# Prompt rows normalized and split inside the last sample unit, gate spreads ahead of the output projection, last values loaded into key buffers

## The chip, the cores and the metric

The kernel runs on one core of one Trainium2 chip. The metric is the device time of one execution in microseconds (us). Lower is better. The kernel before takes 1206.15 us in the median of 3 runs (1203.51 to 1208.47).

## The reference

One layer of a hybrid decoder, for a prompt of 512 rows and for 8 sequences of 8 new rows each (64 sample rows) with 2048 cached positions. All data is float32, the width is 1024.

```python
h = x * (1 + scale1) + shift1                 # shift, scale, gate come from c @ w_ada
proj = h @ w_in                               # q, k, v of the mixers A and B
oa = dilated_mix(q_a, k_a, v_a)               # A: 8 heads of 64, windows (128,1), (512,4), (2048,16)
ob = rms_norm(diff_attention(q_b, k_b, v_b, lam), subln_g) * (1 - lam_init)   # B: 4 heads of 2 x 64
mixed = concat(oa, ob) @ w_o
x = layer_norm(ALPHA * x + gate1 * mixed, ln1_g, ln1_b)
u = (x * (1 + scale2) + shift2) @ w_up + b_up
uc = b_conv + sum(ext[:, j:j + S] * w_conv[j] for j in range(3))
y = (gelu(a) * g) @ w_down + b_down           # a, g are the halves of uc
x = layer_norm(ALPHA * x + gate2 * y, ln2_g, ln2_b)
```

The window caches, shifted by 8 rows, the new key and value rows and the last rows of the convolution are outputs too.

## The kernel before

Each engine has its own instruction stream, written out by hand, with semaphores between them. The work of an engine is done in the order in which it is written. The stages are: modulation and input projection; four prompt attention steps; then the sample stage, which the change touches; the output projection with the first norm; the up-projection with convolution; the down-projection with the second norm.

**The sample stage** is a loop over 16 units `sa` (8 sequences, mixer A and B by turns). A unit of mixer A has three groups of cached keys and values, one of mixer B four, of 512 positions (1 MB) each; the last unit, 15, is of mixer B. SP loads the key groups into three buffers `kraw` (`load_keys`); DVE turns them into `ktg` (`turn_keys`, L1211) and counts `kg_t`. POOL loads the value groups into four buffers `vg` (`load_values`, L480), two in `x_sb` and two in `room`; four transfers of 256 KB make up a group, whose page numbers are read first. TensorE scores keys (L1792), turns probabilities (L1842), and weighs values (`weigh_group`, L1823), which counts `sa_vg`. Behind a unit's groups come its new values (L1871), and `sa_pv` counts the unit; ACT takes the result out (`take_out`, into `o_s`, which lies in `o_all`).

The 60 remaining prompt attention steps `pb` are interleaved, four to a unit (`prompt_step`: scores L1725, turn L1730, weighing L1736); their outputs go to `mixv`, in `mix`. After unit 15's prompt steps, all prompt rows of mixer A and B are there.

**The seam behind the last unit**, up to the output projection, is what the change rewrites. In order, on each engine:

- TensorE: weighing of unit 15, sums of the softmax denominators (L1876 to L1878, `sa_l`), turns of prompt features 0 to 3 (`turn_mixed`, L1886; four transposes of 128x128 each), pick products of the sample rows (L1898, `sa_x`), turns of features 4 to 7, sum of squares of the sample rows (L1904), first half of the first projection tile, `spread_gates` (L1919: eight products that spread the gate columns over rows), then the other nine halves. A half is 24 products of 128x512 (`product`, L1656 to L1658: high x high, high x rest, rest x high, over 8 slices k).
- ACT: `take_out`, root of the prompt's mean squares (L964), high parts of the first half of `w_o` (`high_of_wo`, L969, four of 128x1024), copies of the turned features into `ht` (L975, `mt_a`), four more high parts, root for the sample rows (L980), gate copies (L988, `gb_a`).
- DVE: the sample rows are scaled by the denominators (L1372 to L1379, `sa_n`), the prompt rows of mixer B normalized (L1382, L1385, `rms_ok`), the gate columns expanded (L1390, `mt_d`), the picked sample rows copied and squared (L1406 to L1408), then `split_mixed` (L1398 a cast to the high part, L1399 the rest, `mt_rest`) for features 0 to 3 and 4 to 7, and the norm of the sample rows of mixer B (L1412 to L1418), which counts `sa_fin` to 2: the sample rows are placed.
- POOL: the remainders of eight pieces of `w_o` (`rest_of_piece`, L787), one behind each high part; the first four serve the first half of the columns, the others the second.
- SP: `w_o` in two chunks of 2 MB once all keys are scored (`sa_g`); the copies of x once `sa_pv` is 16; the norm rows and the convolution state (L651, L652) once `sa_fin` is 2. TensorE turns the state in eleven small steps (`st_after`, L1954), the first two right behind the second half of the first tile.

The first tile's halves are j = 0 and j = 1; the rest of the stage is paced by TensorE.

```python
            pe.wait_ge(sa_pt, 2 * len(sa))
            pe.wait_ge(pb_pt, len(pb))
            pe.wait_ge(pb_o, len(pb))
            for f in range(4):
                turn_mixed(f)
```

Of the kernel before, what the change touches and what calls it, by code (L numbers as in the profile page):

```python
# [78 lines left out]
def build(nc, a, o, spill):  # L79
# [6 lines left out]
    with ctx:  # L86
# [87 lines left out]
        mt_high_r = part(room_r, 5120, KT_D * NT).rearrange("p (k t) -> p k t", k=KT_D)  # L174
        stage = mix[:, 0:2048].rearrange("p (b n) -> p b n", b=4)
# [34 lines left out]
        ob_t = part(room, 0, 256)  # L210
        ob_q = part(room, 256, 256)
        ob_r = part(room, 512, 256)
# [3 lines left out]
        ln1 = part(room, 1024, 2048).rearrange("p (w d) -> p w d", w=2)  # L216
# [244 lines left out]

        def load_values(eng, w, g):
# [4 lines left out]
            vs = G % NV  # L467
            if G >= NV:
                eng.wait_ge(sa_vg, G - NV + 1)
            if m == 0 and g < 2:  # L470
                for t in range(4):
                    eng.dma_start(vg[vs][t:P:4, :, :],
                                  win_v[:, 4 * g + t, :].rearrange("(i m) f -> m i f", i=4)).then_inc(vg_in[vs], 16)
            elif m == 0:
                for t in range(2):
                    eng.dma_start(vg[vs][t:P:4, :, :],
                                  win_v[96:128, 8 + 4 * t:12 + 4 * t, :]).then_inc(vg_in[vs], 32)
            else:
                for t, pg in enumerate(page_numbers(eng, b, g)):
                    eng.dma_start(vg[vs][t:P:4, :, :],  # L480
                                  flat_v[1][bass.ds(pg, 1)].rearrange("a (i m) h d -> m (a i) (h d)", i=4))\
                        .then_inc(vg_in[vs], 16)
# [3 lines left out]
        def _(sp):  # L486
# [136 lines left out]
            for w in range(1, len(sa) + 1):  # L623
# [12 lines left out]
                elif here:  # L636
                    load_key_tail(sp, w)
            sp.wait_ge(sa_pv, len(sa) - 1)
# [3 lines left out]
            sp.wait_ge(sa_g, NG[len(sa)])  # L642
            for n in range(FIRST_LATE, FIRST_LATE + 2):
                load_chunk(n)
# [57 lines left out]
        def _(pool):  # L702
# [113 lines left out]
        def _(act):  # L816
# [160 lines left out]
            for q in range(4, 8):  # L977
                high_of_wo(q)
            act.wait_ge(sa_q, 1)
            nc.scalar.activation(ob_q, ob_q, ACT.Sqrt).then_inc(sa_r, 1)  # L980

            act.wait_ge(mt_mm, 8)
            for j in range(8):
# [4 lines left out]
                nc.scalar.activation(g[0:rows, kind, CH * half:CH * half + CH], bk(j % 2)[0:rows, :], ACT.Copy)\  # L988
                    .then_inc(gb_a, 1)

# [49 lines left out]
        def _(dve):  # L1040
# [330 lines left out]
            dve.wait_ge(sa_l, 1)  # L1371
            then(nc.vector.reciprocal(l_s, bk(0)[:, 0:16]))  # L1372
            then(nc.vector.tensor_scalar(lam_s[:, 6:7], diff_c[:, 1:2], lam_s[:, 5:6], diff_c[:, 0:1], ALU.mult, ALU.add))
            l_b = l_s.rearrange("p (b m) -> p b m", m=2)
            then(nc.vector.tensor_scalar(l_b[:, :, 1], l_b[:, :, 1], lam_s[:, 6:7], None, ALU.mult))
            dve.wait_ge(sa_o, 16)
            then(nc.vector.tensor_tensor(o_s, o_s, l_s[:, :, None].to_broadcast([P, 16, P]), ALU.mult))
            o_a = o_s.rearrange("p (b m) d -> p b m d", m=2)[:, :, 0, :]
            nc.vector.tensor_tensor(o_a, o_a, colmask[:, None, :].to_broadcast([P, DB, P]), ALU.mult).then_inc(sa_n, 1)  # L1379

            dve.wait_ge(rms_rt, 1)
# [12 lines left out]
            def split_mixed(f):  # L1394

                dve.wait_ge(mt_a, f + 1)
                high = mt_high_r[:, f, 0:SEQ]
                then(nc.vector.tensor_copy(high, ht[:, f, 0:SEQ]))  # L1398
                nc.vector.tensor_tensor(ht_r[:, f, 0:SEQ], ht[:, f, 0:SEQ], high.bitcast(F32), ALU.subtract).then_inc(mt_rest, 1)  # L1399
# [9 lines left out]
            for f in range(4):  # L1409
                split_mixed(f)  # L1410
            dve.wait_ge(sa_sq, 1)
            nc.vector.tensor_scalar(ob_q, bk(3)[:, 0:256], 1.0 / P, EPS, ALU.mult, ALU.add).then_inc(sa_q, 1)  # L1412
            for f in range(4, KT_D):
                split_mixed(f)
# [165 lines left out]
        def _(pe):  # L1580
# [235 lines left out]
            def weigh_group(w, g):  # L1816
                m, b = sa[w]
                G = NG[w] + g
                pe.wait_ge(vg_in[G % NV], v_count(m, w, g))
                for i in range(4):  # L1820
                    for j in range(4):
                        at = P * g + 32 * i + 16 * (j % 2)
                        last = nc.tensor.matmul(bk(4)[32 * j:32 * j + 16, 0:P], pt_s[:, j // 2, at:at + 16],  # L1823
                                                vg[G % NV][:, i, P * j:P * j + P], start=(g == 0 and i == 0),
                                                stop=False, skip_group_check=True)
                last.then_inc(sa_vg, 1)

# [4 lines left out]
            for w, (m, b) in enumerate(sa):  # L1832
# [27 lines left out]
                else:  # L1860
                    prompt_step(PER * w + 1)
                pe.wait_ge(sa_pt, 2 * w + 2)
                pe.wait_ge(sa_ph, w + 1)
                for g in range(len(groups[m])):
                    weigh_group(w, g)
                    if g == 1 and w + 1 < len(sa):
                        prompt_step(PER * w + 3)
                pe.wait_ge(vn_in, 16 * (w + 1))
# [12 lines left out]
            def turn_mixed(f):  # L1881

                if f >= 4:
                    pe.wait_ge(mt_a, f - 3)
# [254 lines left out]
```

## Time and profile before

| what | value |
|---|---|
| median of 3 runs | 1206.15 us (1203.51 to 1208.47) |
| profiled execution, its own time | 1210.44 us |
| its span | 1208.7 us, mean granted TensorE clock 0.929 |
| busy share PE / DVE / POOL / ACT | 87% / 68% / 38% / 22% |
| chain that ended last, by engine | PE 56%, DVE 16%, DMA 10%, issue 8%, SP's queue 5%, POOL 3% |

The span is the time from the first to the last instruction of the profiled execution. Busy shares are averages over stages with different limits; the chain that ended last is followed back from the last instruction, at each step to what released it.

### The profile page before, as it was taken

Reading aid. Unit: us, or ns where it says so; the run is one execution under the profiler, and the core shown is the slowest. Engines: PE = TensorE matmul, PEld = TensorE weight load, DVE = VectorE, ACT = ScalarE, POOL = GpSimd, SP = SyncE. Lnnn points to the kernel's source line nnn. Section 1 sums busy time; section 2 is a strip of 40 time slices with the busy share of each in tenths; the row PEclk is TensorE's granted clock in tenths of the full one; section 3 lists DMA queues with packets and bytes.
Section 4 is the critical chain, followed back from the end, with each engine's and each line's share of the span. In section 5 each row is a group of like instructions: output and inputs, shape, how many; then the busy total and the mean of one; then the engine's idle time right before and its main releaser. Section 6 shows DMA issues by size and latency. Waiting matters only on the chain.

```text
span 1208.7 us, 24024 instructions
## 1 busy us (share of the span) xinstructions
PE 1049.2 (87%) x9389; PEld 846.9 (70%) x9389; DVE 817.2 (68%) x1485; ACT 271.1 (22%) x600; POOL 462.9 (38%) x587
## 2 busy tenths in 40 slices
PE   4699899985888889878857987999999999999993
PEld 2377567764666556556556767999999999776772
DVE  1637445707878778877557576566757677998868
ACT  0300000011433333334323014223232232101001
POOL 0423224312344434443443006456556565433323
PEclk9699999996989999899957996999999999999997
DMA  8948999869899999999751034556786621413102
GB/s 294 405 144 304 343 334 355 306 213 347 289 337 363 369 310 349 348 364 309 255 202 47 36 96 139 209 209 217 258 287 245 244 70 70 153 58 130 63 3 79
DMA packets 100261, 276.54 MB, mean 229 GB/s; under 512 B 9608, under 2 KB 33174, under 8 KB 96549
## 3 DMA queue, kind: packets, MB, share of 16 engines
q1 hardware_dynamic: 83973, 220.42, 51.8%
q0 software_dynamic: 16128, 54.54, 13.0%
q8 instruction: 75, 1.23, 0.4%
q14 instruction: 37, 0.30, 0.1%
q10 hardware_dynamic: 48, 0.05, 0.0%
HBM read 264.60 MB, written 76.69 MB: 282 GB/s over the span
## 4 chain that ended last, share of the span: by engine, by line
PE 56%; DVE 16%; DMA 10%; issue 8%; SPq 5%; POOL 3%; POOLq 1%; ACT 0%; ACTq 0%; DVEq 0%; PEldq 0%
PE wide L1656 16%; PE wide L1657 15%; PE wide L1658 15%; DMA ring<-in_cache_k 4%; DVE ring L1211 3%; PE wide L1792 3%; DMA ring<-in_w_ada 2%; DMA room<-in_w_ada 2%; SPq L615 2%; DMA ring<-in_w_down 1%; PE wide L1604 1%; SPq L458 1%; DVE ring_r L1135 1%; PE wide L1725 1%; PE wide L1736 1%
## 5 line engine op out<-in xcount | busy, mean ns | idle before, releaser
L787 POOL TENSOR_TENSOR ring_r<-ring,ring_r 128x1024 fp32r<-128x1024 f32 x70 | 183.5, 2629 | 225.8 <-DVE ring_r L1095 205.1
L1656 PE MATMUL wide<-x_sb_r,ring_r 128*128 128x288 f32 x704 | 211.2, 300 | 10.6 <-DVE ht_r L1117 7.5
L1657 PE MATMUL wide<-ht_r,ring_r 128*128 128x288 f32 x704 | 209.4, 297 | 0.0
L1658 PE MATMUL wide<-x_sb_r,ring_r 128*128 128x288 f32 x704 | 208.6, 296 | 0.0
L1658 PE MATMUL wide<-ring_r,ht_r 128*128 128x512 f32 (+1 forms) x400 | 159.0, 398 | 0.0
L1656 PEld LDWEIGHTS wide<-x_sb_r,ring_r 128*128 128x128 f32 x704 | 133.5, 190 | 13.6 <-issue 13.6
L1211 DVE STREAM_TRANSPOSE ring<-ring 128x512 f32<-128x512 f32 x208 | 129.1, 677 | 15.5 <-DMA ring<-in_cache_k 14.8
L1658 PEld LDWEIGHTS wide<-x_sb_r,ring_r 128*128 128x128 f32 x704 | 134.2, 191 | 0.0
L1657 PEld LDWEIGHTS wide<-ht_r,ring_r 128*128 128x128 f32 x704 | 133.9, 190 | 0.0
L1656 PE MATMUL wide<-ring_r,x_sb_r 128*128 128x512 f32 (+1 forms) x240 | 97.8, 407 | 8.8 <-DVE ht_r L1117 8.4
L1657 PE MATMUL wide<-ring_r,x_sb_r 128*128 128x512 f32 (+1 forms) x240 | 95.2, 397 | 0.0
L1656 PE MATMUL wide<-ring_r,ht_r 128*128 128x512 f32 (+1 forms) x220 | 88.2, 401 | 4.1 <-DVE ht_r L1477 1.9
L1658 PEld LDWEIGHTS wide<-ring_r,ht_r 128*128 128x128 f32 (+1 forms) x400 | 72.7, 182 | 21.6
L1657 PE MATMUL wide<-ring_r,ht_r 128*128 128x512 f32 (+1 forms) x220 | 86.8, 394 | 0.0
L1491 DVE SCALAR_TENSOR_TENSOR room<-room,vec_t 128x512 f32<-128x512 f32 x44 | 57.6, 1310 | 42.5 <-ACT room L1012 42.5
L1004 ACT ACTIVATE room<-wide,vec_t 128x576 f32<-128x576 f32 x44 | 32.7, 744 | 207.9 <-PE wide L1658 203.1
L1493 DVE SCALAR_TENSOR_TENSOR room<-room,vec_t 128x512 f32<-128x512 f32 x44 | 69.5, 1578 | 1.6
L1736 PE MATMUL wide<-room 128*128 128x128 f32 x320 | 55.5, 308 | 15.9 <-ACT room L909 11.9
L1792 PE MATMUL wide<-ring,x_sb 128*32 128x128 f32 (+1 forms) x1792 | 64.4, 292 | 4.5 <-DVE ring L1211 2.7
L734 POOL TENSOR_TENSOR ring_r<-ring,ring_r 128x512 fp32r<-128x512 f32 x24 | 34.1, 1425 | 88.3 <-ACT ring_r L835 44.5
L480 POOL DMA_DIRECT2D x_sb<-in_cache_v x64 | 35.2, 550 | 84.7 <-issue 83.6
L1095 DVE CAST ring_r<-ring 128x1024 fp32r<-128x1024 f32 x62 | 41.9, 687 | 36.4 <-DMA ring<-in_w_up 30.2
(239 smaller groups left out, 1977.8 us busy)
## 6 DMA issues: line engine op xcount, KB each, us to landing
ring<-in_cache_k SPq DMA_DIRECT2D x128, 256.0 KB
out_wks<-in_cache_win_k SPq DMA_DIRECT2D x8, 4080.0 KB, 19.0
out_wvs<-in_cache_win_v SPq DMA_DIRECT2D x8, 4080.0 KB, 19.8
ring<-in_w_up SPq DMA_DIRECT2D x22, 1024.0 KB, 7.3
room<-in_w_ada SPq DMA_DIRECT2D x8, 2048.0 KB, 10.2
ring<-in_cache_win_k SPq DMA_DIRECT2D x16, 1024.0 KB
room<-in_cache_v POOLq DMA_DIRECT2D x64, 256.0 KB, 5.7
x_sb<-in_cache_v POOLq DMA_DIRECT2D x64, 256.0 KB, 5.1
```

Of the source, the lines that this page charges most:

```text
L480: eng.dma_start(vg[vs][t:P:4, :, :], flat_v[1][bass.ds(pg, 1)].rearrange("a (i m) h d -> m (a i) (h d)", i=4))\
L734: nc.gpsimd.tensor_tensor(rest, w, high.bitcast(F32), ALU.subtract).then_inc(win_pool, 1)
L787: nc.gpsimd.tensor_tensor(rest, w, high.bitcast(F32), ALU.subtract).then_inc(wl_rest, 1)
L1095: nc.vector.tensor_copy(pair_of(n, slice(k, k + 2))[0], slot(SLOT_OF[n])[:, k:k + 2, :]).then_inc(wl_high, 1)
L1211: last = nc.vector.transpose(ktg[:, G % NK, :, 32 * t:32 * t + 32], kraw[G % NK][:, t, :].rearrange("p (g d) -> p g d", d=32))
L1491: then(nc.vector.scalar_tensor_tensor(out=c_p, in0=u_b[:, k % 2, 1:1 + SEQ], scalar=tap(1), in1=c_p, op0=ALU.mult, op1=ALU.add))
L1493: nc.vector.scalar_tensor_tensor(out=c_p, in0=u_b[:, k % 2, 0:SEQ], scalar=tap(0), in1=c_p, op0=ALU.mult, op1=ALU.add)
L1656: nc.tensor.matmul(out, left[0], right[0], start=first, stop=False)
L1657: nc.tensor.matmul(out, left[0], right[1], start=False, stop=False)
L1658: return nc.tensor.matmul(out, left[1], right[0], start=False, stop=last)
L1736: last = nc.tensor.matmul(bank[:, 0:P], pt_b[:, u % 2, P * kb:P * kb + P], vp[:, kb, m, P * (n // 2):P * (n // 2) + P], start=(kb == 0), s ...
L1792: last = nc.tensor.matmul(bank[32 * nn:32 * nn + 32, at:at + nk], qbd[:, w % 2, g].rearrange("p i q -> p (i q)"), keys[:, g, 0:nk], start= ...
```

## The change

Line numbers of the changed kernel differ from those of the kernel before; each move is told by function name here.

- *Last values.* In unit 15 (`LAST`) groups 1 to 3 of the values are loaded by SP, not POOL, into the key buffer `kraw` that has the number of the group, once the key group in it is turned (`kg_t`). They stand on SP's queue between the new values of units 14 and 15. Since these buffers lie in the slots for `w_o`, the `w_o` loads now wait for all weighings too (`sa_vg`).
- *Prompt rows.* TensorE turns features 0 to 3 before the weighing of unit 15, and 4 to 7 between its groups 1 and 2, once the prompt rows are normalized (`rms_ok`). The turned rows go to banks 5, 6, 1, 7, are copied to free parts of `room` (`mt_part`) in place of `ht`, and are split there. DVE splits 0 to 3, normalizes, expands the gate columns and splits 4 to 7 before it scales the sample rows. ACT copies 0 to 3, takes the root, copies 4 to 7, then does `take_out`.
- *Gates.* The eight spreads stand right behind the sums, ahead of the pick products, in banks 5 and 6. ACT's eight high parts of `w_o` come behind them: one behind each of the gate copies 4 to 7, then four more.
- *Places.* `ob_t`, `ob_q`, `ob_r` move in `room`; the norm rows `ln1` move from `room` to `o_all`.

```diff
+        MT_BANK = [5, 6, 1, 7]
+        def mt_part(t, f):
+            return part(t, 9728 + 512 * f if f < 4 else 512 * (f - 4), 512)
...
-        ln1 = part(room, 1024, 2048).rearrange("p (w d) -> p w d", w=2)
+        ln1 = o_all[:, 0:2 * D].rearrange("p (w d) -> p w d", w=2)
...
+        LAST = 2 * DB - 1
+        def v_home(w, g):
+            G = NG[w] + g
+            if w == LAST and g >= 1:
+                return kraw[G % NK].rearrange("p t d -> p (t d)").rearrange("p (i d) -> p i d", i=4)
+            return vg[G % NV]
...
-            if G >= NV:
+            home, landed = v_home(w, g), v_in(w, g)
+            if w == LAST and g >= 1:
+                eng.wait_ge(kg_t, G + 1)
+            elif G >= NV:
                 eng.wait_ge(sa_vg, G - NV + 1)
...
+            for g in range(1, 4):
+                load_values(sp, LAST, g)
             sp.wait_ge(sa_pv, len(sa) - 1)
             load_new_values(sp, len(sa) - 1)
             sp.wait_ge(sa_g, NG[len(sa)])
+            sp.wait_ge(sa_vg, NG[len(sa)])
             for n in range(FIRST_LATE, FIRST_LATE + 2):
                 load_chunk(n)
...
                 for g in range(len(groups[m])):
-                    load_values(pool, w, g)
+                    if w < LAST or g == 0:
+                        load_values(pool, w, g)
```

ACT, behind the loop over the units:

```diff
-            take_out(len(sa) - 1)
-            act.wait_ge(rms_sq, 1)
-            nc.scalar.activation(rms[:, 1, :], rms[:, 0, :], ACT.Sqrt).then_inc(rms_rt, 1)
...
-            for q in range(4):
-                high_of_wo(q)
-            for f in range(KT_D):
-                act.wait_ge(mt_mm, f + 1)
-                nc.scalar.activation(ht[:, f, 0:SEQ], bk(4 + (f + 1) % 4), ACT.Copy, scale=1.0 if f < 4 else g8[:, 0:1])\
-                    .then_inc(mt_a, 1)
...
+            for f in range(4):
+                take_mixed(f)
+            act.wait_ge(rms_sq, 1)
+            nc.scalar.activation(rms[:, 1, :], rms[:, 0, :], ACT.Sqrt).then_inc(rms_rt, 1)
+            for f in range(4, KT_D):
+                take_mixed(f)
+            take_out(len(sa) - 1)
+            act.wait_ge(mt_mm, KT_D)
             for j in range(8):
                 act.wait_ge(gb_mm, j + 1)
...
+                if j >= 4:
+                    high_of_wo(j - 4)
+            for q in range(4, 8):
+                high_of_wo(q)
```

DVE has the lines of `split_mixed` 0 to 3, of the normalization, of the gate columns and of `split_mixed` 4 to 7 ahead of `dve.wait_ge(sa_l, 1)`, in this order, with no line of theirs behind it. TensorE, unit 15 and behind it:

```diff
                 else:
                     prompt_step(PER * w + 1)
+                    pe.wait_ge(pb_min, len(pb))
+                    pe.wait_ge(pb_pt, len(pb))
+                    for f in range(4):
+                        turn_mixed(f)
...
                     weigh_group(w, g)
...
+                    if g == 1 and w + 1 == len(sa):
+                        pe.wait_ge(rms_ok, 1)
+                        for f in range(4, KT_D):
+                            turn_mixed(f)
...
+            pe.wait_ge(mt_d, 1)
+            pe.wait_ge(mt_a, KT_D)
+            for j in range(8):
...
+                    last = nc.tensor.matmul(bk(5 + j % 2)[0:rows, P * c:P * c + P], col, ident[:, :], start=True, stop=True)
+                last.then_inc(gb_mm, 1)
             pe.wait_ge(sa_o, len(sa))
...
+            pe.wait_ge(gb_a, 8)
             pe.wait_ge(mt_a, KT_D)
             for j in range(2 * (TP + 1)):
...
-                if j == 0:
-                    spread_gates()
```

TensorE's order around the last weighing; `wide` are the accumulator banks, `x_sb`, `room` and `ring` hold values, `mix` the prompt rows. Before, from the last two prompt weighings on:

```order
L1736 MATMUL wide3<-room 128x128 x4
L1730 MATMUL wide3<-ident,room 128x128 x4
L1736 MATMUL wide3<-room 128x128 x4
L1823 MATMUL wide2<-x_sb,ht 16x128 x32
L1823 MATMUL wide2<-room,ht 16x128 x32
L1871 MATMUL wide2<-ht 16x128 x4
L1876 MATMUL wide0<-small,sums 128x16
```

Now:

```order
L1864 MATMUL wide2<-ident,mix 128x128 x4
L1864 MATMUL wide3<-ident,mix 128x128 x4
L1864 MATMUL wide0<-ident,mix 128x128 x4
L1864 MATMUL wide3<-ident,mix 128x128 x4
L1852 MATMUL wide2<-x_sb,ht 16x128 x16
L1852 MATMUL wide2<-ring,ht 16x128 x16
L1864 MATMUL wide2<-ident,mix 128x128 x4
L1864 MATMUL wide3<-ident,mix 128x128 x4
L1864 MATMUL wide0<-ident,mix 128x128 x4
L1864 MATMUL wide3<-ident,mix 128x128 x4
L1852 MATMUL wide2<-ring,ht 16x128 x32
L1918 MATMUL wide2<-ht 16x128 x4
```

Both sets of turns (L1864) have moved into the unit, and three of the four value groups are read from `ring`.

ACT's order behind its last prompt copy; `ring_r<-ring` are the high parts of `w_o`, `mix<-wide` the gate copies. Before:

```order
L914 ACTIVATE o_all<-wide 128x128
L964 ACT_TABLE_LOAD
L964 ACTIVATE rms<-rms 128x16
L969 ACTIVATE ring_r<-ring 128x1024 x4
L975 ACTIVATE ht<-wide 128x512 x4
L975 ACTIVATE ht<-wide,g 128x512 x4
L969 ACTIVATE ring_r<-ring 128x1024 x4
L980 ACTIVATE room<-room 128x256
```

Now:

```order
L1000 ACTIVATE rms<-rms 128x16
L989 ACTIVATE room<-wide,g 128x512 x4
L939 ACTIVATE o_all<-wide 128x128
L1010 ACTIVATE mix<-wide 128x512 x2
L1010 ACTIVATE mix<-wide 64x512 x2
L1010 ACTIVATE mix<-wide 128x512
L995 ACTIVATE ring_r<-ring 128x1024
L1010 ACTIVATE mix<-wide 128x512
L995 ACTIVATE ring_r<-ring 128x1024
```

The high parts of `w_o` have moved from ahead of everything to between and behind the last gate copies.

## Rows read from the trace of the kernel before

**Rows 1.** Windows: length, busy us of PE, PEld, DVE, ACT, POOL, PEclk, DMA share, GB/s.

```profile
596.00:612.00 16.00, 6.00 (x117) 4.58 (x119) 1.63 (x9) 0.60 (x1) 3.52 (x7) 0.76 0.96 351
612.00:628.00 16.00, 9.10 (x71) 7.66 (x64) 10.83 (x7) 7.50 (x11) 10.81 (x4) 0.50 0.56 198
628.00:640.00 12.00, 11.97 (x54) 11.13 (x55) 9.93 (x18) 4.17 (x6) 1.90 (x2) 0.57 0.00 0
```

**Rows 2.** Timeline of PE: start us, us, what, xcount [idle before <-releaser].

```profile
598.66 1.94 PE L1823 MATMUL wide<-x_sb,ht 128*16 128x128 f32 x64
...
605.75 1.91 PE L1823 MATMUL wide<-room,ht 128*16 128x128 f32 x32 [5.15 <-DMA room<-in_cache_v]
611.82 1.91 PE L1823 MATMUL wide<-room,ht 128*16 128x128 f32 x32 [4.17 <-DMA room<-in_cache_v]
...
616.80 3.65 PE L1886 MATMUL wide<-ident,mix 128*128 128x128 f32 x16
627.35 7.04 PE L1898 MATMUL wide<-pick,o_all 128*128 128x32 f32 x32 [6.90 <-DVE o_all L1379]
...
668.25 0.66 PE L1954 MATMUL wide<-ident,room 16*128 16x16 f32 x8
```

**Rows 3.** Timeline of DVE.

```profile
599.81 0.18 DVE L1369 TENSOR_SCALAR rms<-rms 128x16 f32<-128x16 f32 x1
...
619.62 4.39 DVE L1377 TENSOR_TENSOR o_all<-o_all,small 128x2048 f32<-128x2048 f32 x1
...
634.42 0.42 DVE L1406 COPY ht<-wide 128x256 f32<-128x256 f32 x1 [1.89 <-PE wide L1898]
...
636.01 0.69 DVE L1399 TENSOR_TENSOR ht_r<-ht,room_r 128x512 fp32r<-128x512 f32 x1
...
642.47 2.71 DVE L1399 TENSOR_TENSOR ht_r<-ht,room_r 128x512 fp32r<-128x512 f32 x1
...
652.47 1.75 DVE L1416 RECIPROCAL room<-room 128x256 f32<-128x256 f32 x1
...
654.71 0.35 DVE L1418 TENSOR_SCALAR ht<-room,g 128x256 f32<-128x256 f32 x1
```

**Rows 4.** Chain that ended last, 640 to 670.

```profile
654.69 7.96 PE wide L1919 x64
```

**Rows 5.** Timeline of SP's queue (L615 key pages, L453 new values).

```profile
564.51 10.78 SPq L615 DMA_DIRECT2D ring<-in_cache_k  x8
575.97 19.05 SPq L453 DMA_DIRECT2D ht<-ring  x2
```

**Rows 6.** Timeline of ACT.

```profile
616.06 3.88 ACT L969 ACTIVATE ring_r<-ring 128x1024 fp32r<-128x1024 f32 x4
619.85 2.03 ACT L975 ACTIVATE ht<-wide 128x512 f32<-128x512 f32 x4
...
656.09 0.60 ACT L988 ACTIVATE mix<-wide 128x512 f32<-128x512 f32 x1 [13.42 <-PE wide L1919]
```

**Rows 7.** DMA issues, 560 to 760: count, KB each, median us to landing.

```profile
ring<-in_w_o SPq DMA_DIRECT2D x2, 2048.0 KB, 18.1
...
x_sb<-in_x_prompt SPq DMA_DIRECT2D x1, 2048.0 KB, 8.4
...
room<-in_state_conv SPq DMA_DIRECT2D x1, 352.0 KB, 8.3
```

**Rows 8.** Timeline of POOL.

```profile
606.06 0.55 POOL L480 DMA_DIRECT2D room<-in_cache_v  x1 [5.03 <-issue]
617.19 12.32 POOL L787 TENSOR_TENSOR ring_r<-ring,ring_r 128x1024 fp32r<-128x1024 f32 x4 [10.58 <-ACT ring_r L969]
639.60 10.28 POOL L787 TENSOR_TENSOR ring_r<-ring,ring_r 128x1024 fp32r<-128x1024 f32 x4 [10.10 <-ACT ring_r L969]
```

**Rows 9.** Windows, as rows 1, of two microseconds each.

```profile
638.00:640.00 2.00, 1.97 (x8) 1.15 (x7) 1.93 (x5) 2.00 (x3) 0.40 (x1) 0.91 0.00 0
656.00:658.00 2.00, 2.00 (x19) 1.88 (x19) 0.25 (x1) 1.26 (x3) 0.00 (x0) 1.00 0.78 246
```

More of the change, by code:

```diff
@@ L987, in _ @@
                 rows = P if kind == 0 else NS
-                nc.scalar.activation(g[0:rows, kind, CH * half:CH * half + CH], bk(j % 2)[0:rows, :], ACT.Copy)\
+                nc.scalar.activation(g[0:rows, kind, CH * half:CH * half + CH], bk(5 + j % 2)[0:rows, :], ACT.Copy)\
                     .then_inc(gb_a, 1)
+                if j >= 4:
+                    high_of_wo(j - 4)
+            for q in range(4, 8):
+                high_of_wo(q)
+            act.wait_ge(sa_q, 1)
+            nc.scalar.activation(ob_q, ob_q, ACT.Sqrt).then_inc(sa_r, 1)
             for t in range(TP + 1):
@@ L1823, in weigh_group, with turn_mixed @@
                         last = nc.tensor.matmul(bk(4)[32 * j:32 * j + 16, 0:P], pt_s[:, j // 2, at:at + 16],
-                                                vg[G % NV][:, i, P * j:P * j + P], start=(g == 0 and i == 0),
+                                                v_home(w, g)[:, i, P * j:P * j + P], start=(g == 0 and i == 0),
                                                 stop=False, skip_group_check=True)
                 last.then_inc(sa_vg, 1)
+            def turn_mixed(f):
+                if f == 3:
+                    pe.wait_ge(pb_o, len(pb))
+                if f >= 4:
+                    pe.wait_ge(mt_a, f - 3)
+                for t in range(TP):
+                    last = nc.tensor.transpose(bk(MT_BANK[f % 4])[:, P * t:P * t + P], mixv[:, t, P * f:P * f + P], ident[:, :])
+                last.then_inc(mt_mm, 1)
             score_group(0, 0)
@@ L1899, in _ @@
             last.then_inc(sa_x, 1)
-            pe.wait_ge(rms_ok, 1)
-            for f in range(4, KT_D):
-                turn_mixed(f)
             pe.wait_ge(sa_n, 2)
             nc.tensor.matmul(bk(3)[:, 0:256], ones[:, :], ob_q, start=True, stop=True).then_inc(sa_sq, 1)
-            def spread_gates():
-                pe.wait_ge(mt_d, 1)
-                pe.wait_ge(sa_fin, 1)
-                for j in range(8):
-                    which, kind, half = j // 4, (j // 2) % 2, j % 2
-                    rows = P if kind == 0 else NS
-                    if j >= 2:
-                        pe.wait_ge(gb_a, j - 1)
-                    for c in range(4):
-                        f = 4 * half + c
-                        col = mod_t[:, (16, 40)[which] + f, 0:1].to_broadcast([P, P]) if kind == 0 else \
-                            gexp[:, 8 * which + f].rearrange("p b s -> p (b s)")
-                        last = nc.tensor.matmul(bk(j % 2)[0:rows, P * c:P * c + P], col, ident[:, :], start=True, stop=True)
-                    last.then_inc(gb_mm, 1)
+            pe.wait_ge(gb_a, 8)
             pe.wait_ge(mt_a, KT_D)
@@ L1938, in _ @@
                     cols = slice(P * t, P * t + rows)
-                    last = product(bk(4 + j % 4)[0:rows, :], (mt_high_r[:, k, cols], ht_r[:, k, cols]),
+                    low = mt_part(room_r, k)[:, cols] if t < TP else ht_r[:, k, cols]
+                    last = product(bk(4 + j % 4)[0:rows, :], (mt_high_r[:, k, cols], low),
                                    pair_of(n, k), k == 0, k == KT_D - 1)
```

88 lines of the change are left out of this document (42 added, 46 removed).

## The prediction

> **What bounds the kernel now.** All times below are microseconds of the profiled execution before the change, and what the change would do is laid over the same clock. I read the chain of waits first: outside the stretch from 596 to 669 it runs through work that the change leaves alone. Then I read that stretch in windows [rows 1]. TensorE is busy 6.00 of 16.00 us in 596 to 612 and 9.10 of 16.00 in 612 to 628, and its granted clock is near 0.50 from 612 to 640, the lower of its two levels, 1.2 against 2.4 GHz. So this is a seam in which the pipeline runs dry, between the last sample unit and the output projection.
>
> The PE timeline [rows 2] says why. The weighing of the last unit has its first two value groups at 598.66. Its third starts at 605.75 after 5.15 us of waiting and its fourth at 611.82 after 4.17 more, both for values that POOL requested. The turns of the prompt rows (16 in 3.65 us at the low clock) follow at 616.80, behind sums and a long DVE chain: DVE scales the sample rows in 4.39 us, then normalizes the prompt rows, and splits them for the projection while POOL splits weights beside it (2.71 us for a subtraction that takes 0.69 alone) [rows 3]. The chain shows the eight gate spreads, 7.96 us, between the first and the second half of the first projection tile [rows 4]. The second half ends where its state transposes begin, at 668.25 [rows 2]. **From there on every step is paced by TensorE and is the same in both kernels**, so the question is only how early that point, "the handover", comes.
>
> **The change, part by part.**
>
> *Values.* Groups 1 to 3 of the last unit (3 x 4 x 256 KB) go from POOL's queue to SP's, into key buffers that are free once those keys are turned. SP has been idle: two tiny loads fill its 575.97 to 595.02 [rows 5]. It requested the last two key groups, page numbers and waits included, in 10.78, so three value groups take at most 16: out by 592, landed (256 KB of values from POOL took 5.7 to land, 606.06 to the weighing at 611.82 [rows 2, 8]) before 600. That is twelve fewer requests on POOL, which has nothing else then. The two waits, 5.15 + 4.17 = 9.3 us, go. What is late next: after group 1 TensorE waits for the normalized prompt rows.
>
> *Prompt turns, normalization, splits.* At 598.66 TensorE, at full clock, turns features 0 to 3: half of 3.65, so to 600.5. Groups 0 and 1 take 1.94, to 602.4. DVE is free from 600.0 [rows 3]. It gets the first copy from ACT (4 in 2.03 [rows 6]) and splits four features at 0.42 + 0.69, to 604.4. ACT's root, behind its four copies, is hidden beside these splits. Reciprocal and four scalings follow; the scalings have the size of the 0.69 row, 4 x 0.69. So the normalized rows are there at 607.2. **TensorE waits about 4.8 us here**, and on the evidence of 600.6 to 605.75, where a 5.15 us pause halved its pace (32 matmuls in 1.91 against 64 in 1.94 [rows 2]), it continues at the low clock. Four turns 3.65, groups 2 and 3 at 1.91 each, then new values and sums 3.07 (613.73 to 616.80): 617.8. If the clock rises on the way it is 615.6; I take 617. So the nine us won on values are almost spent, and the sums appear about when they did. But turns, normalization and splits are behind us: they cost 3.65 twice and DVE's chain to 652 before. The splits of features 4 to 7 lie beside the weighing and end by 613.
>
> *Weights of the output projection.* They now wait for the last weighing, about 614.5, instead of leaving near 595. Landing was 18.1 beside much other traffic, and 8.4 for 2 MB of x_prompt after it [rows 7]. I take 8: the first half is there at 622.5, the second, behind it, near 628. The two copies of x follow and have until the first gating.
>
> *Gates.* 617 plus 7.96 at full clock [rows 4, 9] is 625. From the fifth on, ACT makes one high part of the weights (3.88 for four, 0.97 each) after each gate copy (0.60) [rows 6]: the first at 622.5 to 623.5, and the last gate spread waits for the copy behind that, so 625.2. POOL's eight remainders start at 623.6, at 2.57 (10.28 for four) to 3.08 each (12.32 for four) [rows 8]: four by 634 to 636, eight by 644.2 to 648.2.
>
> *Sample rows.* DVE's scaling now runs while POOL is idle: 4.39 is both an upper bound and partly a wait; either way it ends before the gates do, so it is worth nothing and costs nothing. The pick matmuls took 7.05 at low clock [rows 2]; at full clock half, 3.5: 628.7. Then comes DVE's short chain, and **this part gets worse**, because POOL is splitting from 623.6 on. Two copies out of the accumulator and the square, 0.42 each alone; the square, with both inputs in SBUF, I take at 2.71, the price of the same kind of operation beside POOL [rows 3]. That gives 632.2, and with the sum of squares 633. The rest is 0.42, ACT's root about as much, the reciprocal 1.75, a product 2.71 and a scaling up to 2.57: the sample rows are placed at 641. Alone it would be 636.5; with the two copies also held 2.71 each it would be 645.6. No row has such a copy beside POOL for long; 0.42 is the nearest row and I take it.
>
> The Trainium skill ("SBUF — State Buffer", section "SBUF: two separate sides") says that the port pair shared by the two engines is held for a whole instruction, and that a DVE operation with two SBUF inputs, or in a two-port mode, is shut out. By it the square, product and scaling wait and the accumulator copies do not, which puts the placing at 641; a view in which everything beside POOL slows alike would give 645.6 and a handover 4.6 later. The trace agrees with it for the subtraction.
>
> *The projection.* Only after the placing does SP ask for the norm rows and the convolution state: 654.71 + 0.35 to the request at 656, then 8.3 to land [rows 3, 7], 9.2 together. So the state is there at **650.2**. The first half starts at 633, needs POOL's fourth remainder, and ends near 638 (one half takes 5.6, from 662.65 to 668.25 [rows 2, 4]). The second needs the eighth, so it ends 1.4 after 644.2 to 648.2, by 645.6 to 649.6. The state transposes are behind it. The handover is the later of the two: **about 650, against 668.25**. Before, the state landed at 664.3 and hid behind the gates. Now it and POOL set the end together.
>
> **Sum.** 668.25 - 650.2 = 18 us. The profiled execution took 1210.44 (span 1208.7), 4.3 above the median of the runs, 1206.15. Taking 18 from each gives 1192.4 for a profiled run and **1188** for the median. Bounds: with nothing held beside POOL and its faster pace, 645.7, a gain of 22.6, 1183.5. With sample copies held, and gates and picks partly at the low clock, 656, a gain of 12, 1194.
>
> **Rivals.** About 0.5%, 6 us, is what a measurement of this kernel can tell from no change.
>
> *A. The clock stays low through gates and picks* (0.13). For it: 0.50 all through 612 to 638 before, and only 0.91 in 638 to 640 after eleven us of continuous work [rows 1, 9]. Against: the pauses of 621 and the long ones around 606 and 611 are gone. Then the gates take 16 (to 633), POOL starts at 628.6 and ends by 649 to 653, picks end at 640, the placing is at 652, the state at 661: a gain of 4 to 8, 1198 to 1202.
>
> *B. POOL alone ends the seam* (0.2): the DVE operations slip between its instructions, and the handover is 645.7 to 647: 1184.
>
> *C. The change does not do its main thing* (0.04): SP's value loads land late, since DMA was nearly saturated (share 0.96 [rows 1]), so TensorE waits as before, and the weights, now behind the weighing, come at 625: within 6 of before.
>
> *D. Slower, by the clock* (0.03). TensorE is paced by POOL and by the state from 633 to 650, with pauses of 2 to 5 us, and if it then runs all ten halves at the low clock (10.3 instead of 5.6), the placing is as in A and 8 x 4.7 = 38 us come on top: 1235. It decides from about five halves on. Against it: before, DVE's splits stopped TensorE again and again until 650, and the gates from 654.69 on still ran at 1.00 [rows 9]; and the halves behind the handover have no waits inside.
>
> The forecast itself has 0.6. The likeliest is 1188. The range goes down to 1182 (B, and a low draw of the median) and up to 1199 (most of A). Faster 0.88, same 0.08, slower 0.04.
>
> **What would show it.** Right: value groups 2 and 3 weighed with no DMA wait; one pause of 4 to 5 us before features 4 to 7; gates from about 617; POOL's splits from about 624 to 646; the first state transposes near 650, their wait ending on the state's landing or on POOL. From there to the end, the same length as before (540 us). Wrong: weighings still waiting for DMA, a gate spread of 16 us, or a granted clock under 0.9 after 655.

## The result, and the profile after

The changed kernel takes 1186.79 us in the median of 4 runs (1185.78 to 1189.57) against 1206.85 for the kernel before in the same comparison: 0.9832 of its time, with a 95% interval of 0.981 to 0.9853. That is 20.1 us less; 18 were forecast. The profiled execution took 1186.03, with a span of 1184.3 and a mean granted clock of 0.940. One execution of a kernel further down (e5) came out at 1236.95 us with a granted clock of 0.816, against 1181.18 to 1189.89 for its other five; the ratios leave it out.

Windows of the changed kernel over the seam, with the columns of [rows 1]:

```profile
596.00:612.00 16.00, 11.37 (x178) 9.81 (x177) 12.42 (x27) 6.60 (x11) 0.00 (x0) 0.79 0.04 5
612.00:628.00 16.00, 13.00 (x100) 11.79 (x100) 6.47 (x9) 12.21 (x16) 8.81 (x4) 0.94 1.03 393
628.00:640.00 12.00, 11.70 (x48) 9.09 (x46) 10.43 (x6) 0.42 (x1) 10.50 (x5) 0.93 0.53 137
```

TensorE is busy 11.37 of 16 us where it was busy 6.00, and 13.00 where it was 9.10, at a granted clock of 0.94 and not 0.50. DMA, saturated from 596 to 612 before, is idle there now (0.04) and saturated from 612 to 628.

Timeline of PE, the rows that answer to [rows 2] and [rows 4]:

```profile
595.42 1.91 PE L1864 MATMUL wide<-ident,mix 128*128 128x128 f32 x16
597.26 1.07 PE L1852 MATMUL wide<-x_sb,ht 128*16 128x128 f32 x32
598.15 1.06 PE L1852 MATMUL wide<-ring,ht 128*16 128x128 f32 x32
603.84 3.67 PE L1864 MATMUL wide<-ident,mix 128*128 128x128 f32 x16 [4.63 <-DVE mix L1412]
607.44 2.76 PE L1852 MATMUL wide<-ring,ht 128*16 128x128 f32 x64
...
611.83 2.03 PE L1939 MATMUL wide<-ident,mod_t 128*128 128x128 f32 x16
...
619.64 1.09 PE L1939 MATMUL wide<-ident,room 128*64 128x128 f32 x8 [0.90 <-ACT mix L1010]
620.66 3.76 PE L1945 MATMUL wide<-pick,o_all 128*128 128x32 f32 x32
626.52 1.22 PE L1948 MATMUL wide<-room,ones 128*128 128x256 f32 x2 [2.10 <-DVE room L1441]
...
642.97 0.81 PE L1981 MATMUL wide<-ident,room 16*128 16x16 f32 x8 [2.76 <-DMA room<-in_state_conv]
```

Both waits on values are gone, and one wait of 4.63 us for the normalized prompt rows stands in their place. Behind it the four turns run at half pace (3.67 against 1.91 for the same 16). The gates follow the sums without a gap, and the first state transposes start at 642.97 after 2.76 us of waiting for the state.

I call the **seam** the time from the end of the last prompt weighing, taken as the start of what follows it on TensorE, to the first state transposes. Before it is 668.25 - 598.66 = 69.59 us, now 642.97 - 595.42 = 47.55: 22.0 us less. The last prompt weighing ends 3.2 us earlier too, in a part of the program that the change leaves as it was. I put that down to the two executions: their own times, 1210.44 and 1186.03, lie 24.4 apart, the medians 20.1, and in the ten profiles of this document this point lies anywhere from 593.12 to 598.90. What follows the seam is as long as before: 1208.7 - 668.25 = 540.5 and 1184.3 - 642.97 = 541.3.

The chain of waits of the changed kernel in the seam:

```profile
610.31 7.72 DMA ring<-in_w_o
618.05 1.06 ACT ring_r L995
...
631.34 2.38 DVE ht L1447
...
634.61 8.32 DMA room<-in_state_conv
```

Two landings hold it now: `w_o`, asked for only once the last values are weighed, and the state, asked for only once the sample rows are placed.

Timeline of POOL and of DVE behind the picks:

```profile
619.19 19.31 POOL L812 TENSOR_TENSOR ring_r<-ring,ring_r 128x1024 fp32r<-128x1024 f32 x8 [37.96 <-ACT ring_r L995]
```

```profile
624.46 0.42 DVE L1439 COPY ht<-wide 128x256 f32<-128x256 f32 x1 [8.02 <-PE wide L1945]
624.80 0.41 DVE L1440 COPY room<-wide 128x256 f32<-128x256 f32 x1
625.25 1.21 DVE L1441 TENSOR_TENSOR room<-room 128x256 f32<-128x256 f32 x1
...
628.68 1.75 DVE L1445 RECIPROCAL room<-room 128x256 f32<-128x256 f32 x1 [0.48 <-ACT room L1017]
630.47 0.83 DVE L1446 TENSOR_TENSOR room<-room 128x256 f32<-128x256 f32 x1
631.34 2.37 DVE L1447 TENSOR_SCALAR ht<-room,g 128x256 f32<-128x256 f32 x1
```

Four more rows of DVE before the change, the first two beside POOL's splits and the last two with POOL at rest:

```profile
617.60 1.99 DVE L1375 TENSOR_SCALAR small<-small,lam_s 128x8 f32<-128x8 f32 x1
...
624.05 3.25 DVE L1379 TENSOR_TENSOR o_all<-o_all,colmask 128x1024 f32<-128x1024 f32 x1
...
635.21 0.42 DVE L1408 TENSOR_TENSOR room<-room 128x256 f32<-128x256 f32 x1
...
654.25 0.42 DVE L1417 TENSOR_TENSOR room<-room 128x256 f32<-128x256 f32 x1
```

POOL splits from 619.19 to 638.50. Beside it the two copies out of the accumulator take 0.42 and 0.41, as they do alone. Of the four operations within SBUF (the on-chip memory of the engines) the reciprocal takes 1.75, as alone; the square, the product and the scaling take 1.21, 0.83 and 2.37 where they take 0.42, 0.42 and 0.35 alone.

### The profile page after: what moved, and what is told of

Same layout as the page of the kernel before. It is cut to its first block, busy times and chain, and to the rows that moved or that the text cites. A ratio compares the mean times of both kernels' runs of the same rounds, so it can differ in the third digit from the quotient of the medians.

```text
span 1184.3 us, 24024 instructions
## 1 busy us (share of the span) xinstructions
PE 1035.5 (87%) x9389; PEld 836.7 (71%) x9389; DVE 811.4 (69%) x1485; ACT 271.0 (23%) x600; POOL 453.3 (38%) x575
## 4 chain that ended last, share of the span: by engine, by line
PE 57%; DVE 15%; DMA 10%; issue 9%; SPq 4%; POOL 3%; POOLq 1%; ACT 0%; ACTq 0%; DVEq 0%; PEldq 0%
PE wide L1685 16%; PE wide L1687 15%; PE wide L1686 15%; DVE ring L1239 3%; DMA ring<-in_cache_k 3%; DMA ring<-in_w_ada 2%; DMA room<-in_w_ada 2%; PE wide L1821 2%; PE wide L1633 1%; DMA ring<-in_w_down 1%; PE wide L1765 1%; SPq L636 1%; SPq L464 1%; DVE ring_r L1163 1%; PE wide L1754 1%
## 5 line engine op out<-in xcount | busy, mean ns | idle before, releaser
L812 POOL TENSOR_TENSOR ring_r<-ring,ring_r 128x1024 fp32r<-128x1024 f32 x70 | 180.4, 2585 | 243.2 <-DVE ring_r L1123 205.2
L1239 DVE STREAM_TRANSPOSE ring<-ring 128x512 f32<-128x512 f32 x208 | 129.3, 679 | 15.7 <-DMA ring<-in_cache_k 15.2
L1687 PE MATMUL wide<-ring_r,ht_r 128*128 128x512 f32 (+1 forms) x336 | 133.2, 396 | 0.0
L1685 PE MATMUL wide<-ring_r,ht_r 128*128 128x512 f32 (+1 forms) x220 | 88.2, 401 | 4.7 <-DVE room L1541 2.3
L1686 PE MATMUL wide<-ring_r,ht_r 128*128 128x512 f32 (+1 forms) x220 | 86.5, 393 | 0.0
L1687 PE MATMUL wide<-ring_r,room_r 128*128 128x512 f32 (+1 forms) x204 | 80.2, 393 | 0.0
L1687 PEld LDWEIGHTS wide<-ring_r,ht_r 128*128 128x128 f32 (+1 forms) x336 | 60.2, 179 | 18.8
L1765 PE MATMUL wide<-room 128*128 128x128 f32 x320 | 55.5, 308 | 15.5 <-ACT room L934 12.3
L1685 PEld LDWEIGHTS wide<-ring_r,x_sb_r 128*128 128x128 f32 (+1 forms) x240 | 43.7, 182 | 30.0 <-issue 17.2
```

The source lines that it names most:

```text
L812: nc.gpsimd.tensor_tensor(rest, w, high.bitcast(F32), ALU.subtract).then_inc(wl_rest, 1)
L1239: last = nc.vector.transpose(ktg[:, G % NK, :, 32 * t:32 * t + 32], kraw[G % NK][:, t, :].rearrange("p (g d) -> p g d", d=32))
L1685: nc.tensor.matmul(out, left[0], right[0], start=first, stop=False)
L1686: nc.tensor.matmul(out, left[0], right[1], start=False, stop=False)
L1687: return nc.tensor.matmul(out, left[1], right[0], start=False, stop=last)
L1765: last = nc.tensor.matmul(bank[:, 0:P], pt_b[:, u % 2, P * kb:P * kb + P], vp[:, kb, m, P * (n // 2):P * (n // 2) + P], start=(kb == 0), s ...
```

## The experiments

Eight kernels ran, each in 6 runs: its profiled one and five rounds against the kernel before. Medians of the same kernel move by a few us between executions, so each seam, measured as above, is read together with the median. The ratios all refer to the kernel before, in two comparisons: one with the changed kernel once more, e3, e4 and e5 (median before 1208.57), one with e1, e2, e6 and e7 (1209.49).

| kernel | median us | ratio (95%) | seam us |
|---|---|---|---|
| before | | 1 | 69.59 |
| changed, first profile | 1186.79 | 0.9832 (0.981 to 0.9853) | 47.55 |
| changed, once more | 1187.47 | 0.982 (0.979 to 0.9851) | 50.50 |
| e1, values back on POOL | 1189.57 | 0.985 (0.982 to 0.9879) | 47.47 |
| e2, values alone | 1194.56 | 0.99 (0.9866 to 0.9934) | 54.56 |
| e3, gates back | 1189.79 | 0.9849 (0.9818 to 0.988) | 52.31 |
| e4, state early | 1185.43 | 0.9811 (0.978 to 0.9842) | 44.28 |
| e5, filler | 1186.85 | 0.9798 (0.9763 to 0.9833) | 47.61 |
| e6, reordered | 1179.82 | 0.9759 (0.9731 to 0.9787) | 44.33 |
| e7, reordered with filler | 1178.76 | 0.976 (0.973 to 0.979) | 38.81 |

**The changed kernel once more.**

> The changed kernel once more, as the measure for the three beside it. Both theories: 0.983 of the kernel before, 1186 to 1188 us; handover (first state transposes, L1981) 47.5 us after the last prompt weighing ends, with a wait of about 2.8 on the landing of the convolution state.

The total came as expected, 1187.47. The seam did not: 50.50 where 47.5 was expected, with a wait of 3.91 for the state. Timeline of PE in this execution:

```profile
619.33 1.09 PE L1939 MATMUL wide<-ident,room 128*64 128x128 f32 x8 [0.96 <-ACT mix L1010]
620.34 5.43 PE L1945 MATMUL wide<-pick,o_all 128*128 128x32 f32 x32
628.50 1.22 PE L1948 MATMUL wide<-room,ones 128*128 128x256 f32 x2 [2.73 <-DVE room L1441]
645.84 0.92 PE L1981 MATMUL wide<-ident,room 16*128 16x16 f32 x8 [3.91 <-DMA room<-in_state_conv]
```

Two windows of it, with the granted clock before the last two columns:

```profile
620.00:622.00 2.00, 2.00 (x19) 1.83 (x17) 0.00 (x0) 2.00 (x4) 2.00 (x2) 1.00 1.05 385
622.00:624.00 2.00, 2.00 (x12) 2.00 (x11) 0.00 (x0) 1.92 (x3) 2.00 (x2) 0.53 1.06 408
```

The picks, 3.76 us in the first profile, take 5.43 here: the clock falls to its lower level in the middle of them, without a pause just there. What follows the seam is longer too, 544.2 against 541.3. So one seam differs by some 3 us between executions of one kernel, and smaller differences of a single seam prove nothing.

**Gates back.**

```diff
-            pe.wait_ge(mt_d, 1)
-            pe.wait_ge(mt_a, KT_D)
-            for j in range(8):
...
-            pe.wait_ge(gb_a, 8)
+            def spread_gates():
+                pe.wait_ge(mt_d, 1)
+                pe.wait_ge(sa_fin, 1)
+                for j in range(8):
...
+                if j == 0:
+                    spread_gates()
```

The spreads use banks 0 and 1 again in place of 5 and 6, and the high halves of `w_o` and the root of the sample rows stand ahead of the gate copies on ACT, not between them.

> The gate spreads and their copies go back between the two halves of the first projection tile; everything else stays. My theory: the spreads fill a pause before the picks, so undoing costs less than their 8 us: picks start some 4 us earlier but at the low clock, the first half ends near 636 on the changed kernel's clock, spreads to 644, second half to 649, handover 3 to 7 us later: 1190 to 1194. Rival 1, the spreads were fully on the path and are fully hidden now: 8 us, 1195. Rival 2, POOL and the state set the end anyway: within 1 us, 1187.

Timeline of PE:

```profile
619.16 7.00 PE L1930 MATMUL wide<-pick,o_all 128*128 128x32 f32 x32 [4.61 <-DVE o_all L1431]
...
636.73 1.95 PE L1947 MATMUL wide<-ident,mod_t 128*128 128x128 f32 x16
...
650.08 0.66 PE L1982 MATMUL wide<-ident,room 16*128 16x16 f32 x8
```

Without the spreads TensorE waits 4.61 us for the scaled sample rows, and the picks behind the pause take 7.00 us in place of 3.76 to 5.43. The seam is 52.31, 1.8 to 4.8 us longer than in the two profiles of the changed kernel, and the median 2.3 us longer. The spreads, 7.6 us here (636.73 to 644.37), had been moved into a hole of 4.6 us, and the picks behind them run at full clock for at least a part of their time. That speaks against the 8 us of rival 1. How much less moving them is worth is not shown: the differences, 1.8 to 4.8 in the seam and 2.3 in the median, point to the low end of the theory's 3 to 7, but the intervals overlap and the smaller one lies within the 3 us by which one kernel differs from itself. Rival 2, within 1 us, is therefore not excluded by the times; its reason doesn't hold, since the state was no longer waited for here.

**State early.**

```diff
+            sp.wait_ge(pb_exp, len(pb))
+            sp.dma_start(st_r, a["state_conv"][0].rearrange("b j f -> (b j) f")).then_inc(st_in, 16)
             sp.wait_ge(sa_fin, 2)
...
-            sp.dma_start(st_r, a["state_conv"][0].rearrange("b j f -> (b j) f")).then_inc(st_in, 16)
```

> The convolution state is requested right behind the copies of x (about 615) and not after the placing of the sample rows. My theory: the handover is held by this landing and by nothing else for the last 2.8 us; without it the second half's end, paced by POOL, is the handover: 2.5 to 2.8 us earlier, 1184. Rival: the wait is replaced by another (the norm rows, DVE's first gating, or a bank) and the time stays at 1187.

```profile
625.13 1.22 PE L1949 MATMUL wide<-room,ones 128*128 128x256 f32 x2 [2.08 <-DVE room L1442]
639.22 0.67 PE L1982 MATMUL wide<-ident,room 16*128 16x16 f32 x8
```

```profile
617.82 19.29 POOL L813 TENSOR_TENSOR ring_r<-ring,ring_r 128x1024 fp32r<-128x1024 f32 x8 [38.47 <-ACT ring_r L996]
```

The wait is gone, and the seam is 44.28, 3.3 us shorter than the shorter of the two profiles. Of these, 0.9 were there before the first half began, since the gates began at 15.5 us of the seam and not at 16.4; 2.4 are left for the state, as the theory had it. What the theory had wrong is the next bound. POOL ends its last remainder at 637.11, 42.2 us into the seam, and TensorE waits for nothing between the sum of squares at 625.13 and the handover: it is its own pace, at the low clock for the first ten products or so, that sets the end. The state needs nothing that the placing of the sample rows frees. Its part of `room` held the last two value groups and buffers of the prompt steps in the kernel before, all used up long before the placing, so by the layout that kernel could have asked early too; it was not tried there. The median moved by 2.0 us, with overlapping intervals; the seam speaks for the theory, the medians only don't contradict it.

**Filler.**

```diff
                     if g == 1 and w + 1 == len(sa):
+                        for x in range(36):
+                            nc.tensor.transpose(bk(0)[:, P * (x % 4):P * (x % 4) + P], mixv[:, x % 4, 0:P], ident[:, :])
                         pe.wait_ge(rms_ok, 1)
```

> 36 turns of an already turned prompt block into bank 0 fill TensorE's pause of 4.6 us before features 4 to 7; their result is read by nobody, the output is the reference's. My theory, the clock: turns 4 to 7 take 1.9 and not 3.67, the two weighings 2.1 and not 2.8, so the sums, the request for w_o and POOL's start come 2 to 2.6 us earlier and so does the end: 1184 to 1185. Rival: the placing chain and landings are bound elsewhere, or the filler delays the turns: 1187 or more.

```profile
602.61 4.15 PE L1913 MATMUL wide<-ident,mix 128*128 128x128 f32 x36
607.31 1.97 PE L1864 MATMUL wide<-ident,mix 128*128 128x128 f32 x16 [0.55 <-DVE mix L1412]
609.21 1.94 PE L1852 MATMUL wide<-ring,ht 128*16 128x128 f32 x64
...
621.74 5.51 PE L1947 MATMUL wide<-pick,o_all 128*128 128x32 f32 x32
...
646.51 0.66 PE L1983 MATMUL wide<-ident,room 16*128 16x16 f32 x8 [3.23 <-DMA room<-in_state_conv]
```

The cost of the clock after the pause is what was said for the turns: 1.97 in place of 3.67. The weighings take 1.94, but without a filler they take 2.76, 2.47, 3.00, 1.94 and 1.99 in five profiles, so the filler is not needed for their pace. POOL starts at 620.26 - 598.90 = 21.4 us of the seam, where it starts at 23.8, 23.5 and 22.9 in the two profiles of the changed kernel and in e4: 1.5 to 2.4 us earlier, and not 2 to 2.6. But the picks fell to the low clock in this execution (5.51), the state was waited for again, and the seam is 47.61. The theory's first half holds in the main; its gain at the end does not show here, and the median, 1186.85, is the rival's.

**Values back on POOL.** In `v_home`, `v_in`, `load_values` and the weighing, `w == LAST` becomes a condition that never holds, POOL loads all groups, SP's three loads and the wait of `w_o` on `sa_vg` go.

> The changed kernel with value groups 1 to 3 of the last unit back on POOL in their own buffers, and w_o requested as before, without waiting for the weighings. My theory: the early values are worth almost nothing, since TensorE waits for the normalized rows anyway; the fourth group lands about 13 us after the last prompt weighing, where it is weighed at 12 to 15 in the changed kernel, and w_o comes earlier in exchange: handover within 1 us of the changed kernel's 47.5 to 50.5, 1187. Rival: the two waits of together 9.3 us come back into the path: 1195.

```profile
606.46 3.67 PE L1860 MATMUL wide<-ident,mix 128*128 128x128 f32 x16 [4.70 <-DVE mix L1408]
...
612.34 1.07 PE L1848 MATMUL wide<-room,ht 128*16 128x128 f32 x32 [0.37 <-DMA room<-in_cache_v]
...
645.46 0.66 PE L1977 MATMUL wide<-ident,room 16*128 16x16 f32 x8 [2.73 <-DMA room<-in_state_conv]
```

The two waits of 5.15 and 4.17 us don't come back: 0.37 us is left of them. The values arrive while TensorE waits for the normalized rows (4.70 us, as in the changed kernel) and turns them. The seam is 47.47 against 47.55. **In the changed kernel the early values are worth nothing that can be seen**; the median is 2.1 us above the changed kernel's of the other comparison, within the intervals. This run undoes two things at once that pull against each other, though neither by more than a us: the sums begin at 15.7 us of the seam and not at 15.0, but `w_o`, asked for at 594.55 again, is no longer waited for, so that the last gate spreads wait 0.21 and not 0.90.

**Values alone.** The kernel before, with the additions to SP's queue, `v_home` and the `w_o` wait of the change and nothing else of it.

> The kernel before, with only the values of the last unit moved to SP's queue and the key buffers (and w_o behind the weighings). Without the rest of the change there is no normalization in the way. My theory: sums and sample scaling come 9 to 10 us earlier, POOL's splits wait for w_o, so part is lost behind its landing: handover 9 to 14 us earlier than the 69.6 of before, 1194 to 1199. Rival: late weights eat all of it, 1206. With the run that undoes the same part: if both are large the parts overlap, if this is large and that is nothing, the prompt part has taken the same time over.

```profile
603.51 7.03 PE L1917 MATMUL wide<-pick,o_all 128*128 128x32 f32 x32 [2.72 <-DVE o_all L1398]
...
648.09 0.66 PE L1973 MATMUL wide<-ident,room 16*128 16x16 f32 x8
```

```profile
599.91 2.29 DVE L1396 TENSOR_TENSOR o_all<-o_all,small 128x2048 f32<-128x2048 f32 x1
...
616.36 2.72 DVE L1418 TENSOR_TENSOR ht_r<-ht,room_r 128x512 fp32r<-128x512 f32 x1
```

The seam is 54.56, 15.0 us shorter than before, and the ratio 0.99. The median, 1194.56, is at the theory's low end; the seam went 1 us beyond its 9 to 14. The 15.0 are more than the 9.3 us of waits, for two reasons. Without the pauses TensorE does the weighings and sums at full clock, so the sums are done 12.8 us earlier in the seam (598.85 - 593.53 = 5.3 against 616.80 - 598.66 = 18.1): 3.5 more than the waits. And POOL's splits, which now wait for `w_o`, no longer meet the three steps that scale the sample rows: 0.23, 2.29 and 1.22 us where they took 1.99, 4.39 and 3.25, or 5.9 less. Together the picks begin 18.7 us earlier. POOL's splits still meet the prompt splits (2.72), and between picks and handover some 4 of these are lost again. So the same part is worth 15 us of seam on the kernel before and nothing on the rest of the change, whose other parts alone (e1) give 22. **The parts overlap almost fully: either takes most of the other's gain.** The prompt rows alone, without values and gates, were not tried; how the 22 us divide between prompt rows and gates is known only as far as e3 tells it.

**Reordered, without and with the filler.**

```diff
-            for q in range(8):
+            for q in [2, 3, 5, 6, 7]:
                 rest_of_piece(q)
...
+            for q in [0, 1]:
+                rest_by_dve(q)
             dve.wait_ge(sa_x, 1)
...
             nc.vector.tensor_tensor(ob_q, ob_t, ob_t, ALU.mult).then_inc(sa_n, 1)
+            for q in [4]:
+                rest_by_dve(q)
...
+                if j == 0:
+                    pe.wait_ge(sa_n, 2)
+                    nc.tensor.matmul(bk(3)[:, 0:256], ones[:, :], ob_q, start=True, stop=True).then_inc(sa_sq, 1)
```

On top of it the state comes early, as in e4, and its first turn waits only until DVE has read the sum of squares, and no longer for the placing of the sample rows (`sa_fin`). The placing was done before that turn in both profiles (at 635.6 and 633.3), so this did not shorten the seams.

> The changed kernel with the state requested early, the sum of squares behind the first half and not before it, and DVE taking three of POOL's eight remainders (pieces 0, 1, 4). My theory: the first half starts right behind the picks, 3 us earlier, and POOL ends 3 us earlier: handover about 41.5 after the last prompt weighing against 47.5, so 1181. Rival: DVE's pieces and POOL's exclude each other for whole instructions, so the remainders end no earlier and the time is that of the early state alone, 1184.

> The same with the filler turns in TensorE's pause. My theory: another 2.4 us, since sums, w_o and POOL come earlier, 1179. Rival: as with the filler alone, the picks fall to the low clock and give it back, 1181.

Timeline of PE with the filler, then of DVE and POOL:

```profile
618.34 3.76 PE L1959 MATMUL wide<-pick,o_all 128*128 128x32 f32 x32
627.51 0.59 PE L1989 MATMUL wide<-room,ones 128*128 128x256 f32 x2
...
634.31 0.66 PE L2001 MATMUL wide<-ident,room 16*128 16x16 f32 x8
```

```profile
616.82 1.22 DVE L1440 TENSOR_TENSOR ring_r<-ring,ring_r 128x1024 fp32r<-128x1024 f32 x1 [2.82 <-ACT ring_r L997]
...
624.65 3.42 DVE L1440 TENSOR_TENSOR ring_r<-ring,ring_r 128x1024 fp32r<-128x1024 f32 x1
...
639.10 1.29 DVE L1488 TENSOR_TENSOR room<-wide,mix 128x512 f32<-128x512 f32 x2 [4.56 <-DMA o_all<-in_ln_b]
```

```profile
619.73 12.95 POOL L814 TENSOR_TENSOR ring_r<-ring,ring_r 128x1024 fp32r<-128x1024 f32 x5 [34.86 <-ACT ring_r L997]
```

Both beat the kernel before: 0.9759 (0.9731 to 0.9787) and 0.976 (0.973 to 0.979), and the medians, 1179.82 and 1178.76, came as expected. The changed kernel of the other comparison has 0.982 with an interval from 0.979, just where theirs end. **What the new order adds to the early state is not shown**: e4's interval (0.978 to 0.9842) overlaps, and the seam of e6 is 44.33 against e4's 44.28 and against the 41.5 expected. There the picks took 5.84 in place of 3.76, which is 2.1 of the 2.8 us missing.

DVE makes a remainder in 1.22 us ahead of POOL and in 3.42 beside it. POOL ends its five 13.0 us after its start, where eight take 19.3; it is done 38.6 us into the seam in e6 against 42.2 in e4, so the exclusion that the rival expected costs some, but not all. In the seams e6 and e7 differ by 5.5 us (44.33 and 38.81), of which 2.1 are the picks (5.84 and 3.76). The medians differ by 1.1, so **the filler is not shown to be worth anything in the total**. What sets the clock during the picks stays open; it was not tried.

Behind the handover of e7 DVE waits 4.56 us, on the chain that ended last, for the norm rows `ln1`, which SP still asks for only once the sample rows are placed. That is the next late request; what it would give to send it earlier was not tried.

## Why the prediction was right

The median, 1186.79, lies 1.2 below the forecast of 1188. Point by point, in us of the seam, with the prediction's clock less 598.66. In the main the mechanism came as it was told, with the waits in that order; what was off are sizes, and they were off in one direction:

- *Waits on values, and what is late next.* Said: both go, and a pause of 4.8 takes their place. Measured: 4.63, for the normalized prompt rows. That the nine us are "almost spent" is what e1 shows.
- *Low clock behind the pause.* Right for the turns (3.67). The weighings came back to full clock on the way (2.76 for the two, taken as 3.82): gates began at 16.4, where 18.3 was taken and 17 the lower bound. This is the first term that was too large, by 1.9. Only 1.3 of it reached the picks (at 25.2, said 26.5), since the last gate spreads waited for `w_o`.
- *`w_o`.* Asked for at 14.9 (15.8 said) and landed in 7.7 (8 said). POOL ran from 23.8 to 43.1, said 24.9 and up to 49.5. POOL's pace, 2.41 a piece, was below both rows taken, 2.57 and 3.08.
- *Sample rows.* The copies out of the accumulator are not held beside POOL (0.42, 0.41). By the rule cited of the Trainium skill ("SBUF — State Buffer", section "SBUF: two separate sides") they should not be, and that the square and the product were held for part of an instruction only agrees too: the wait is for what is left of POOL's instruction, 0.8 and 0.4 in this execution, and not each time the 2.0 on top of 0.69 that [rows 3] gave. The scaling, which follows the product at once, was held 2.0 (2.37, said up to 2.57). This is the second term that was too large, by 3.4 for square and product together: placing ended at 38.3, said 42.3. The prediction's 636.5 for this chain with nothing held is a slip: its own rows (0.42 three times, 0.8, 0.42, 0.42, 1.75, 0.42, 0.35) give 634.1. The forecast does not use it.
- *State.* 8.3 to land, as said, and waited for, 2.76. Said: state and POOL set the end together, at 51.5. Measured: the state alone, at 47.55. POOL's last remainder held TensorE for 0.30 us, and the second half was over at 44.8; e4 shows that it is the state, and that without it TensorE's own pace sets the end and not POOL.
- *Sum.* 18 against 22.0 in the profiled seams and 20.1 in the medians. Of the 4.0 that the seam was forecast too long, all lie ahead of the placing; from there to the landing 9.2 was said and 9.3 measured. That the median is 1.2 from the forecast is in part luck: the second profile of the same kernel has a seam of 50.50, 1 us from the forecast 51.5, and the first is 4.0 away. The sign of both errors is the same: bounds from rows of the kernel before, in which POOL and DVE met more often, were too pessimistic here.

The rivals: A did not occur as told, since gates ran at full clock in every profile, but the picks were partly at the low clock in four of the seven profiles that have the gates ahead of them. B, POOL alone at the end, did not occur in the changed kernel, nor in e4, where POOL is done 2.1 us before the handover. C and D did not occur; the transfers of the values hid as said.

One thing the prediction did not see: it gave the values a price of 9.3 us and said rightly that they lose it to the next wait, but e2 shows that alone they are worth 15 us of seam, since they also keep TensorE's clock up for the weighings and sums and pull `w_o` behind the weighing and so POOL's splits out of the sample scaling.

## What to carry to other kernels

Price a part of a change twice: alone on the old kernel and undone on the new one. Here the same part gave 15 us of seam and nothing, and only the pair shows that a simpler change, without it, does the same as far as these runs can tell. When a seam is shortened, look for requests that wait for more than they need: the state's load waited for the placing of the sample rows, which frees nothing of its place, and that came to matter only when the work in front of it shrank. And a wait of a few us costs TensorE twice, once in waiting and once in the pace behind it (here 4.63 us and another 1.7 in the turns). Filling such a wait gave back the pace but no time in the total that these runs could show.

## What was not expected of the hardware

The granted clock fell in the middle of 32 small products of 32 columns each that followed one another without a pause, in some executions and not in others: 3.76, 4.46, 5.43, 5.51 and 5.84 us for the same group, each behind a pause of 0.2 to 1.0 us for the last gate copy. What the clock had to do with the work in front was not tried. And POOL's split of a 128x1024 piece takes 3.08 us on average in one group of these traces and 2.38 to 2.59 in the others. What DVE does beside it differs among them, and DVE's own operations take up to 2.77 us there where they take 0.69 alone; that the one makes the other was not tried by itself.
